# Attention's value product moved behind the next branch's scores, in one step of a woven TensorE queue

## The chip, the cores and the metric

The kernel runs on one core of a Trainium2 chip. The metric is the device time of one execution in microseconds (us), the median of several runs. One more execution was taken by the hardware profiler; its rows are quoted below. TensorE (PE in the rows), VectorE (DVE), ScalarE (ACT) and SyncE (SP) each work through a queue of their own in order, and wait for each other by semaphores.

## What is computed

The model is one hybrid layer (gated delta rule for four heads, sparse attention for four heads, a feed-forward block) and a second one (gated linear attention, a state space part, product-key experts), over 512 positions of width 1024. The change touches only the first layer's sparse attention. Per block of 128 queries and per head it has three branches, each a masked softmax, weighted by a gate, times values:

```python
s_c = jnp.einsum('bqhd,bkd->bqhk', qb, k_cmp) * scale        # 31 compressed keys
p_c = masked_softmax(s_c, mask_c[None, :, None, :])
o_c = jnp.einsum('bqhk,bkd->bqhd', p_c, v_cmp)
...                                                          # o_s: selected blocks, o_w: window
return gb[..., 0:1] * o_c + gb[..., 1:2] * o_s + gb[..., 2:3] * o_w
```

With 512 positions all eight selectable blocks are chosen and the window covers everything before a query, so both larger branches run over all keys up to the query's block. Beside it runs the gated delta rule in chunks, whose triangular system is inverted by repeated small products, and the modulation `mod = silu(c) @ ada_w + ada_b`.

## The kernel before

The mixer stage lies at 290 to 552 us of the profiled span. Three generators per engine write it down: the delta rule (`gdn_*`), attention (`attn_*`), and, inside attention's steps, the modulation (`ada_*`). `weave` draws one step of the delta rule and 0.42 steps of attention in turn (`RATES`), alike on TensorE, VectorE and ScalarE, so each engine's queue is one fixed mixture.

The delta rule has four lanes (one per chunk of 128 positions). Each lane is a chain in which TensorE makes four 128x128 products into the lane's PSUM bank (line 1102) and VectorE combines the bank with what is in SBUF (lines 1208, 1210, 1212, the matrices Y, XT and X, called `qkv` in the rows). Lanes are visited in turn, so TensorE can be three or four products ahead of VectorE. Behind the lanes follows a serial chain (`CHAIN`) over the chunks.

Attention has 48 branches: 4 query blocks `mt`, 4 heads, 3 branches `br`. At step n

- TensorE makes the scores of branch n (lines 1349 and 1352 or 1355, `bank4` or `bank5` in turn) and transposes the probabilities of branch n-2 into `bank6` (line 566);
- VectorE takes the maximum of branch n's scores (line 1415), then normalizes branch n-1 (the last of it on line 146 or 151), and does three, three or two products of a modulation tile (lines 146 and 151, `mod_acc`, in `ada_ve`);
- ScalarE takes the exponential of branch n (line 1381), then copies the transposed branch n-2 into `PC` or `PT` (lines 1390, 1392).

Every third step (n = 5, 8, ... 50) also closes a group g = (n-5)/3, which is one head of one query block. TensorE then waits for the copy of the group's last branch (`at_pt` at 3g+3), multiplies the three probability tiles with the values into a part of `bank7` (line 554 from line 1343; 1 + 2(mt+1) products), and for g > 0 ahead of it makes the modulation's two 128x1 products (`ada_pe`). ScalarE copies the result (line 1398) behind its exponential and its copy of branch n-2; that copy of branch n-2 waits for the product too, since it overwrites `PC`. VectorE subtracts what the copy lost (line 1406, `lower`), and TensorE waits for that of the group before.

A 32-bit product runs as two passes, so a product of the program is two rows' worth of the trace's counts. The stage ends when all engines have arrived (`arrive(..., 3)`), and the next one starts from there.

Of the kernel before, what the change touches and what calls it, by code (L numbers as in the profile page):

```python
# [268 lines left out]
def _build(nc, D, ctx):  # L269
    s = Sems(nc, ctx)  # L270
# [3 lines left out]
    def sb(name, shape, dt=F32, c=ctx):  # L274
        return c.enter_context(nc.sbuf_tensor(name, shape, dt))
# [24 lines left out]
    pm = bank[7]  # L300
# [21 lines left out]
    with ExitStack() as ar:  # L322
# [3 lines left out]
        tm = sb("tm", [128, 4, 276], F32, ar)  # L326
        kcmp = sb("kcmp", [128, 32], F32, ar)
        vcmp = sb("vcmp", [32, 128], F32, ar)
# [11 lines left out]
        with ExitStack() as a2:  # L340
# [4 lines left out]
            PC = sb("PC", [32, 128], F32, a2)  # L345
            PT = [sb(f"PT{j}", [128, 512], F32, a2) for j in range(2)]
# [49 lines left out]
    with ExitStack() as ar:  # L396
# [36 lines left out]
        mt = [sb(f"mt{j}", [128, 512], F32, ar) for j in range(3)]  # L433
# [118 lines left out]
    def mm(p, out, pairs, start=True, stop=True, check=True):  # L552
        for i, (l, r) in enumerate(pairs):
            ins = p.e.matmul(out, l, r, start=start and i == 0, stop=stop and i == len(pairs) - 1,  # L554
                             skip_group_check=not check)
        return ins
# [7 lines left out]
    def tr(p, out, in_):  # L564
        k = in_.shape[0]
        return p.e.transpose(out, in_, ident[0:k, 0:k])  # L566
# [152 lines left out]
    def ada_pe(p, i):  # L719
        p.wait_ge(s("ada_sum"), i + 1)  # L720
        for j in range(2):
            c = 2 * i + j
            ins = mm(p, pm[:, c:c + 1], [(mod_acc(i)[:, 128 * j:128 * j + 128], C["ones"][:, 0:1])], check=False)
        p.then_inc(ins, s("ada"))
# [600 lines left out]
    def span_of(n):  # L1325
        return 31 if branches[n][2] == 0 else 128 * (branches[n][0] + 1)

    def attn_pe(p):
        for n in range(51):
            if n >= 5 and n % 3 == 2:  # L1330
                g = (n - 5) // 3
                mt = g // 4
                if g:
                    p.wait_ge(s("at_lo"), g)
                else:
                    p.wait_ge(s("me_h"), 1)
                if g:
                    ada_pe(p, 7 + g)
                p.wait_ge(s("at_pt"), 3 * g + 3)
                pairs = [(vcmp[0:31, :], PC[0:31, 0:128])]  # L1340
                pairs += [(tm[:, j, 128 * b:128 * b + 128], PT[b][:, 128 * j:128 * j + 128])
                          for b in range(2) for j in range(mt + 1)]
                p.then_inc(mm(p, pm[:, 128:256], pairs, check=False), s("at_pv"))
            if n < 48:
                mt, h, br = branches[n]
                qT, ps, L = nsq[:, h, 128 * mt:128 * mt + 128], bank[4 + n % 2], span_of(n)
                if n >= 2:
                    p.wait_ge(s("at_ex"), n - 1)
                p.e.matmul(ps[:, 0:L], qT, kcmp[:, 0:31] if br == 0 else kk2[:, br - 1, 0:L], start=True, stop=False,
                           skip_group_check=True)  # L1350
                if br == 0:
                    ins = p.e.matmul(ps[:, 0:31], ident, C["cmpadd"][:, 31 * mt:31 * mt + 31], start=False, stop=True,
                                     skip_group_check=True)
                else:
                    ins = p.e.matmul(ps[:, L - 128:L], ident, C["causal"], start=False, stop=True, skip_group_check=True)
                p.then_inc(ins, s("at_s"))
            if 2 <= n < 50:
                m = n - 2
                P = Pb[m % 3]
                p.wait_ge(s("at_p"), m + 1)  # L1360
                if m:
                    p.wait_ge(s("at_pt"), m)
                if branches[m][2] == 0:
                    ins = tr(p, bank[6][0:31, 0:128], P[:, 0:31])
                else:
                    for j in range(branches[m][0] + 1):
                        ins = tr(p, bank[6][:, 128 * j:128 * j + 128], P[:, 128 * j:128 * j + 128])
                p.then_inc(ins, s("at_t"))
            yield
        p.wait_ge(s("at_lo"), 16)  # L1370
        ada_pe(p, 23)
# [103 lines left out]
    def mixer_pe(p):  # L1475
        arrive(p, 2)
        run(meta_pe(p))
        together((gdn_pe(p), RATES[0]), (attn_pe(p), RATES[1]))
# [1807 lines left out]
```

## Time and profile before

| | us |
|---|---|
| median of 3 runs | 3661.42 |
| lowest, highest | 3661.38, 3662.98 |
| the profiled execution's own time | 3658.62 |
| its span | 3656.7 |
| the mixer stage in it, 290.0 to 551.9 | 261.9 |

The profiled execution took 3658.62 us, of which 3656.7 are the span from the first instruction to the last and 1.9 lie around it. It is 2.8 us under the median. Over the whole span TensorE is busy for 95%, VectorE for 55% and ScalarE for 33%; these are means over stages with different limits, and the mixer stage is read by itself. A row of the timeline gives the start, the duration, the engine, the line, the operation and its tiles, and in brackets how long the engine had been idle before it and what ended that.

### The profile page before, as it was taken

What the parts mean: (1) busy time and instruction counts of PE and PEld (TensorE: products, weight loads), DVE (VectorE), ACT (ScalarE), POOL (GpSimd) and SP (SyncE); (2) the same over time, 40 slices, a digit from 0 to 9 for tenths busy, and PEclk for the clock granted to TensorE, in tenths of its full rate; (3) what the DMA queues carried; (4) which work ended last, traced back from release to release, by engine and by line L of the source; (5) the groups of instructions that cost most, each with busy time, mean ns of one, the idle gap of its engine ahead of it and who ended that gap; (6) DMA issues with size and microseconds to landing.
All of it is one profiled execution on the core that took longest, in us unless ns stands there. A gap on an engine that the chain in (4) does not pass through costs nothing.

```text
span 3656.7 us, 43203 instructions
## 1 busy us (share of the span) xinstructions
PE 3478.0 (95%) x18062; PEld 2951.6 (81%) x18062; DVE 1998.5 (55%) x3622; ACT 1217.0 (33%) x1598; POOL 0.2 (0%) x4
## 2 busy tenths in 40 slices
PE   6997879999998999999899989999999999999998
PEld 5886877878788789888787878888888888888887
DVE  6427853747434435667533288687785444444443
ACT  2234132222233324555422224444444322222222
POOL 0000000000000000000000000000000000000000
PEclk9888988999999989999998999999999999999998
DMA  5222212232321241122143333544545665555551
GB/s 222 76 88 74 81 47 92 82 109 82 119 82 54 67 158 70 58 81 92 65 176 117 147 132 125 185 157 160 186 164 179 222 233 184 196 196 184 194 196 59
DMA packets 211314, 474.64 MB, mean 130 GB/s; under 512 B 10272, under 2 KB 141856, under 8 KB 175024
## 3 DMA queue, kind: packets, MB, share of 16 engines
q1 hardware_dynamic: 208960, 463.89, 36.7%
q10 hardware_dynamic: 2160, 7.99, 0.6%
q8 instruction: 143, 2.34, 0.3%
q14 instruction: 51, 0.42, 0.0%
HBM read 380.61 MB, written 91.23 MB: 129 GB/s over the span
## 4 chain that ended last, share of the span: by engine, by line
PE 83%; DVE 9%; ACT 4%; DMA 1%; issue 1%; SPq 0%; ACTq 0%; DVEq 0%
PE bank L554 78%; PE bank L617 2%; DVE mod_acc L151 1%; DVE wl L509 1%; PE bank L2346 1%; ACT wh L502 1%; PE bank L624 1%; ACT sgm L2414 1%; DMA x<-in_xT 1%; PE bank L566 0%; DVE st L1415 0%; PE bank L1102 0%; PE bank L2355 0%; ACT P L1381 0%; ACT sgm L2418 0%
## 5 line engine op out<-in xcount | busy, mean ns | idle before, releaser
L554 PE MATMUL bank<-hh,wh 128*128 128x512 f32 (+1 forms) x2512 | 982.5, 391 | 37.1 <-DVE wl L509 13.3
L509 DVE TENSOR_TENSOR wl<-ring,wh 128x2048 fp32r<-128x2048 f32 (+2 forms) x250 | 557.1, 2229 | 817.2 <-ACT wh L502 817.1
L554 PE MATMUL bank<-hl,wh 128*128 128x512 f32 (+1 forms) x2512 | 954.8, 380 | 0.0
L554 PE MATMUL bank<-hh,wl 128*128 128x512 f32 (+1 forms) x2512 | 952.6, 379 | 0.0
L502 ACT ACTIVATE wh<-ring 128x2048 fp32r<-128x2048 f32 (+2 forms) x250 | 465.4, 1862 | 1077.9 <-PE bank L554 1070.8
L554 PEld LDWEIGHTS bank<-hh,wh 128*128 128x128 f32 x2512 | 483.8, 193 | 134.3 <-issue 32.4
L554 PEld LDWEIGHTS bank<-hl,wh 128*128 128x128 f32 x2512 | 483.1, 192 | 91.6 <-issue 6.3
L554 PEld LDWEIGHTS bank<-hh,wl 128*128 128x128 f32 x2512 | 482.0, 192 | 92.3
L554 PE MATMUL bank<-pl,wh 128*128 128x512 f32 x1024 | 403.5, 394 | 0.0
L554 PE MATMUL bank<-ph,wh 128*128 128x512 f32 x1024 | 401.4, 392 | 0.0
L554 PE MATMUL bank<-ph,wl 128*128 128x512 f32 x1024 | 397.3, 388 | 0.0
L554 PEld LDWEIGHTS bank<-ph,wh 128*128 128x128 f32 x1024 | 192.2, 188 | 45.0
L554 PEld LDWEIGHTS bank<-ph,wl 128*128 128x128 f32 x1024 | 192.2, 188 | 43.0
L554 PEld LDWEIGHTS bank<-pl,wh 128*128 128x128 f32 x1024 | 192.5, 188 | 38.2
L2803 ACT ACTIVATE stage<-bank 128x512 f32<-128x512 f32 x128 | 140.5, 1106 | 102.6 <-PE bank L554 102.6
L554 PE MATMUL bank<-wh,hh 128*128 128x256 f32 (+2 forms) x520 | 155.4, 299 | 0.0
L554 PE MATMUL bank<-wh,hl 128*128 128x256 f32 (+2 forms) x520 | 150.9, 290 | 0.0
L554 PE MATMUL bank<-wl,hh 128*128 128x256 f32 (+2 forms) x520 | 150.9, 290 | 0.0
L2884 ACT ACTIVATE gst<-bank 128x512 f32<-128x512 f32 x128 | 75.3, 590 | 204.3 <-PE bank L554 148.2
L2823 DVE TENSOR_SCALAR Ah<-cst,ijw 128x128 f32<-128x128 f32 x512 | 142.4, 342 | 0.0
L554 PEld LDWEIGHTS bank<-Bh,Ah 128*128 128x128 f32 x1024 | 133.1, 191 | 10.6
L554 PE MATMUL bank<-Bh,Ah 128*128 128x128 f32 x1024 | 133.8, 274 | 0.0
(466 smaller groups left out, 4096.2 us busy)
## 6 DMA issues: line engine op xcount, KB each, us to landing
ring<-in_v SPq DMA_DIRECT2D x68, 1024.0 KB, 4.9
ring<-in_u SPq DMA_DIRECT2D x64, 1024.0 KB, 5.5
gelu_spill<-gst SPq DMA_DIRECT2D x128, 256.0 KB, 2.4
weight_spill<-stage SPq DMA_DIRECT2D x32, 1024.0 KB, 9.0
gv<-gelu_spill SPq DMA_DIRECT2D x64, 512.0 KB, 4.4
wv<-weight_spill SPq DMA_DIRECT2D x64, 512.0 KB, 5.7
ring<-in_ada SPq DMA_DIRECT2D x24, 1024.0 KB, 5.0
ring<-in_wup SPq DMA_DIRECT2D x22, 1024.0 KB, 4.8
```

The lines of the kernel that those rows point to most:

```text
L151: return e.scalar_tensor_tensor(out=out, in0=a, scalar=x, in1=b, op0=op0, op1=op1)
L502: a.then_inc(a.e.activation(wh[q % 2][:, 0:n], ring[k % 4][:, 0:n], ACT.Copy), s("whi"))
L509: v.then_inc(v.e.tensor_tensor(wl[q % 2][:, 0:n], ring[k % 4][:, 0:n], wh[q % 2][:, 0:n].bitcast(F32), S_), s("parts"))
L554: ins = p.e.matmul(out, l, r, start=start and i == 0, stop=stop and i == len(pairs) - 1, skip_group_check=not check)
L617: ins = p.e.matmul(out[:, j:j + 1], sq[:, 128 * j:128 * j + 128], C["ones"][:, 0:1], start=start and j == 0, stop=stop, skip_group_check=True)
L624: ins = p.e.matmul(out[:, 128 * j:128 * j + 128], r[:, j:j + 1].to_broadcast([128, 128]), ident, start=j == 0, stop=True, skip_group_check ...
L2346: p.then_inc(p.e.matmul(bank[7][:, :], l, r, start=True, stop=True), s("ss_mm"))
L2414: ins = a.e.activation(sg[:, h, :], bank[3 + h // 4][:, 128 * (h % 4):128 * (h % 4) + 128], ACT.Abs, bias=nac[:, j, 8 * g + h:8 * g + h + 1])
L2803: a.then_inc(a.e.activation(stage[half][:, :, 4 * (q % 16):4 * (q % 16) + 4].rearrange("p j t -> p t j"), quad(bank[5 + t % 3][:, :]), ACT ...
L2823: ins = v.e.tensor_scalar(Ah[t % 3][:, z, :], C["iota"], ijw[:, 0, k:k + 1], ijw[:, 2, k:k + 1], ALU.is_equal, M)
L2884: a.then_inc(a.e.activation(gst[t % 2][:, :], bank[t % 4][:, :], ACT.Gelu_apprx_tanh), s("ge_u"))
```

## The change

In `attn_pe` the part that closes a group stands behind the step's scores and transposes instead of ahead of them. Nothing else is edited: the products, the tiles, the semaphores and what is waited for are the same, and so are the queues of VectorE, ScalarE and SyncE, row for row. Up to step 47 the closing part comes behind branch n's scores and branch n-2's transpose; at step 50 there are neither scores nor a transpose, and the order is as it was.

```diff
     def attn_pe(p):
         for n in range(51):
-            if n >= 5 and n % 3 == 2:
-                g = (n - 5) // 3
-                mt = g // 4
-                if g:
-                    p.wait_ge(s("at_lo"), g)
-                else:
-                    p.wait_ge(s("me_h"), 1)
-                if g:
-                    ada_pe(p, 7 + g)
-                p.wait_ge(s("at_pt"), 3 * g + 3)
-                pairs = [(vcmp[0:31, :], PC[0:31, 0:128])]
-                pairs += [(tm[:, j, 128 * b:128 * b + 128], PT[b][:, 128 * j:128 * j + 128])
-                          for b in range(2) for j in range(mt + 1)]
-                p.then_inc(mm(p, pm[:, 128:256], pairs, check=False), s("at_pv"))
             if n < 48:
...
                 p.then_inc(ins, s("at_t"))
+            if n >= 5 and n % 3 == 2:
+                g = (n - 5) // 3
+                mt = g // 4
...
+                p.then_inc(mm(p, pm[:, 128:256], pairs, check=False), s("at_pv"))
             yield
```

In the rows below `kk,nsq` are scores, `cst` with them the mask that is added, `cst,P` the transpose, `mod_acc` the modulation, `PC,vcmp` and `PT,tm` the value product. On TensorE, at step 32 (group 9, the third query block), there stood before, from the lane product ahead of the step to the one behind it:

```order
L1102 MATMUL bank<-qkv,AT 128x128 x4
L554 MATMUL bank<-cst,mod_acc_1 128x1 x2
L554 MATMUL bank<-PC,vcmp 128x128
L554 MATMUL bank<-PT,tm 128x128 x6
L1349 MATMUL bank<-kk,nsq 128x384
L1355 MATMUL bank<-cst 128x128
L566 MATMUL bank<-cst,P 31x128
L1102 MATMUL bank<-XT,Y 128x128 x4
```

and there stands now:

```order
L1102 MATMUL bank<-qkv,AT 128x128 x4
L1335 MATMUL bank<-kk,nsq 128x384
L1341 MATMUL bank<-cst 128x128
L566 MATMUL bank<-cst,P 31x128
L554 MATMUL bank<-cst,mod_acc_1 128x1 x2
L554 MATMUL bank<-PC,vcmp 128x128
L554 MATMUL bank<-PT,tm 128x128 x6
L1102 MATMUL bank<-XT,Y 128x128 x4
```

The scores and the transpose have changed places with the modulation's products and the value product; the lane products around them stay.

On TensorE at step 47 (group 14), behind the last products of the lanes (`XT,kbe` and `qkv,XT`) and ahead of the serial chain's first ones (`AT,kd` and `mix,AT`), there stood before:

```order
L1102 MATMUL bank<-qkv,XT 128x128 x4
L554 MATMUL bank<-cst,mod_acc_0 128x1 x2
L554 MATMUL bank<-PC,vcmp 128x128
L554 MATMUL bank<-PT,tm 128x128 x8
L1349 MATMUL bank<-kk,nsq 128x512
L1355 MATMUL bank<-cst 128x128
L566 MATMUL bank<-cst,P 31x128
L1102 MATMUL bank<-AT,kd 128x128 x4
```

and there stands now:

```order
L1102 MATMUL bank<-qkv,XT 128x128 x4
L1335 MATMUL bank<-kk,nsq 128x512
L1341 MATMUL bank<-cst 128x128
L566 MATMUL bank<-cst,P 31x128
L554 MATMUL bank<-cst,mod_acc_0 128x1 x2
L554 MATMUL bank<-PC,vcmp 128x128
L554 MATMUL bank<-PT,tm 128x128 x8
L1102 MATMUL bank<-AT,kd 128x128 x4
```

Here too the same pieces have changed places, and the chain's products stay behind both.

## Rows read from the trace of the kernel before

**Rows 1.** Windows of the stage: busy time per engine, granted clock, DMA share.

```profile
core 0: us, PE busy (x) PEld busy (x) DVE busy (x) ACT busy (x) POOL busy (x), PEclk, DMA share, GB/s
360.15:409.41 49.26, 44.30 (x354) 41.50 (x355) 45.62 (x125) 10.46 (x41) 0.00 (x0) 1.00 0.24 86
409.41:452.39 42.98, 37.13 (x280) 33.79 (x280) 35.21 (x94) 8.48 (x30) 0.00 (x0) 0.96 0.22 74
452.39:496.10 43.71, 37.99 (x289) 33.68 (x290) 33.02 (x88) 13.65 (x38) 0.00 (x0) 1.00 0.24 79
496.10:523.30 27.20, 23.56 (x113) 21.64 (x114) 9.00 (x25) 6.01 (x12) 0.00 (x0) 0.63 0.20 69
```

**Rows 2.** Waits of VectorE, 290 to 530 us: total, times, longest.

```profile
DVE st L1415 <- PE bank L1355: 26.3, 12, 9.5
```

**Rows 3.** Waits of TensorE, 409 to 505 us: total, times, longest.

```profile
PE bank L554 <- ACT PT L1392: 7.8, 6, 2.0
```

**Rows 4.** Timeline around the close of group 9, TensorE, VectorE and ScalarE.

```profile
422.77 0.50 PE L554 MATMUL bank<-cst,mod_acc 128*128 128x1 f32 x4
...
424.18 0.48 ACT L1392 ACTIVATE PT<-bank 128x384 f32<-128x384 f32 x1
...
424.71 0.48 PE L554 MATMUL bank<-PC,vcmp 31*128 31x128 f32 x2 [1.44 <-ACT PT L1392]
...
426.57 0.81 PE L1349 MATMUL bank<-kk,nsq 128*128 128x384 f32 x2
...
427.54 1.06 PE L1102 MATMUL bank<-XT,Y 128*128 128x128 f32 x8
...
427.63 0.56 DVE L1415 TENSOR_REDUCE st<-bank 128x1 f32<-128x384 f32 x1 [1.22 <-PE bank L1355]
...
428.42 0.58 ACT L1381 ACTIVATE P<-bank,st 128x384 f32<-128x384 f32 x1 [3.76 <-DVE st L147]
...
429.43 0.29 DVE L1406 TENSOR_TENSOR hl<-bank,hh 128x128 fp32r<-128x128 f32 x1 [0.27 <-ACT hh L1398]
```

**Rows 5.** Timeline, VectorE's maximum at the close of groups 1, 4, 8, 11 and 12.

```profile
318.76 0.29 DVE L1415 TENSOR_REDUCE st<-bank 128x1 f32<-128x128 f32 x1 [3.03 <-PE bank L1355]
...
362.42 0.42 DVE L1415 TENSOR_REDUCE st<-bank 128x1 f32<-128x256 f32 x1 [0.34 <-PE bank L1355]
...
413.92 0.56 DVE L1415 TENSOR_REDUCE st<-bank 128x1 f32<-128x384 f32 x1 [2.81 <-PE bank L1355]
...
455.53 0.69 DVE L1415 TENSOR_REDUCE st<-bank 128x1 f32<-128x512 f32 x1 [1.54 <-PE bank L1355]
...
470.56 0.69 DVE L1415 TENSOR_REDUCE st<-bank 128x1 f32<-128x512 f32 x1 [2.09 <-PE bank L1355]
```

**Rows 6.** Timeline around the close of group 13.

```profile
480.18 0.59 ACT L1392 ACTIVATE PT<-bank 128x512 f32<-128x512 f32 x1
...
480.82 0.48 PE L554 MATMUL bank<-PC,vcmp 31*128 31x128 f32 x2 [0.46 <-ACT PT L1392]
...
483.12 1.02 PE L1349 MATMUL bank<-kk,nsq 128*128 128x512 f32 x2
...
484.31 1.06 PE L1102 MATMUL bank<-qkv,XT 128*128 128x128 f32 x8
...
484.40 0.69 DVE L1415 TENSOR_REDUCE st<-bank 128x1 f32<-128x512 f32 x1 [2.09 <-PE bank L1355]
```

**Rows 7.** Timeline from the end of the lanes into the serial chain.

```profile
496.10 0.98 PE L554 MATMUL bank<-cst,mod_acc 128*128 128x1 f32 x4 [0.99 <-ACT AT L1178]
...
503.17 1.06 PE L1102 MATMUL bank<-AT,kd 128*128 128x128 f32 x8
503.26 0.69 DVE L1415 TENSOR_REDUCE st<-bank 128x1 f32<-128x512 f32 x1 [9.50 <-PE bank L1355]
...
506.80 0.68 DVE L1283 COPY St<-bank 128x512 f32<-128x512 f32 x1
...
507.54 1.16 PE L1102 MATMUL bank<-St,Y 128*128 128x128 f32 x8 [1.67 <-DVE St L1283]
```

More of the change, by code:

```diff
@@ L1368, in attn_pe @@
                 p.then_inc(ins, s("at_t"))
+            if n >= 5 and n % 3 == 2:
+                g = (n - 5) // 3
+                mt = g // 4
+                if g:
+                    p.wait_ge(s("at_lo"), g)
+                else:
+                    p.wait_ge(s("me_h"), 1)
+                if g:
+                    ada_pe(p, 7 + g)
+                p.wait_ge(s("at_pt"), 3 * g + 3)
+                pairs = [(vcmp[0:31, :], PC[0:31, 0:128])]
+                pairs += [(tm[:, j, 128 * b:128 * b + 128], PT[b][:, 128 * j:128 * j + 128])
+                          for b in range(2) for j in range(mt + 1)]
+                p.then_inc(mm(p, pm[:, 128:256], pairs, check=False), s("at_pv"))
             yield
```

## The prediction

> **What bounds the kernel now.** The change is confined to the mixer stage, so I read that stage alone, first its windows, then the waits, then the timeline around the close of a group.
>
> In the windows [rows 1] no engine has the stage to itself. From 360.15 to 409.41, VectorE is busy 45.6 of 49.3 us (93%) and TensorE 44.3. From 409.41 to 452.39 VectorE falls to 35.2 of 43.0 (82%), from 452.39 to 496.10 to 33.0 of 43.7 (76%), while TensorE is busy 37.1 and 38.0. So the second and third window each hold 8 to 11 us in which VectorE stands still, and there is no other engine that is full. That is the sign of two engines that wait for each other.
>
> The waits name the place. VectorE stands 26.3 us in 12 pieces ahead of line 1415, the maximum over a branch's scores, until TensorE's mask product of line 1355 [rows 2]. In the other direction TensorE stands 7.8 us in 6 pieces ahead of line 554 until ScalarE's copy into `PT` [rows 3]. The two belong together, as the close of group 9 shows [rows 4]: TensorE has ended the modulation's two products at 423.2 and then stands 1.44 us until the copy that began at 424.18. The value product holds it from 424.71 to 426.5, and only then come the scores, which took nothing from that copy and could have been made in the gap. VectorE, out of other work, stands 1.22 us until they are there, at 427.63.
>
> **The change part by part.** No instruction is added or removed, and only TensorE's queue is reordered. What counts is what each engine then waits for. I first follow group 9.
>
> *Scores.* They need an exponential two branches back, long done. They start where the modulation's products started, 422.8, and take 1.0 us (426.57 to 427.54, with the mask and the transpose that follow) [rows 4]. They are ready by 423.8, so VectorE's 1.22 us are gone whole. What is late next on VectorE is line 1406, which waits for ScalarE's copy of the value product.
>
> *Transpose.* It takes about 0.1 us of the queue and waits for `bank6`, that is for the same `PT` copy as the value product. It costs the value product 0.1 us.
>
> *Modulation.* Its two products, 0.5 us long and about 0.4 us of the queue [rows 4], come behind that wait now, where before they filled time ahead of it. That is the price of the change: the value product starts 0.5 to 0.6 us later against the copy than before. It ends at 427.0 to 427.1 instead of 426.5. The lane product behind it starts at about 427.1 where it was 427.54, a gain of 0.4 to 0.5 us, because the score block has left this side of the wait.
>
> *ScalarE and line 1406.* ScalarE's exponential began at 428.42 and now begins 1.22 us earlier, at 427.2; its copy of branch n-2 and the copy of the product follow from 427.8. The product is there at 427.1. So the later value product is hidden by the maximum and the exponential, by 0.7 us; if that cover were gone, every us would be one of VectorE's. Line 1406 comes 1.22 us earlier and still waits 0.27.
>
> *Who is late next.* VectorE gains 1.2 us per such group and TensorE's own order only 0.4 to 0.5, but TensorE had 1.44 us of gap in it, which it now fills with the scores and gives up. In the second window TensorE is busy 37.1 of 43.0 us [rows 1], so 5.9 us can be given up before it is the bound.
>
> The other groups, by VectorE's wait [rows 4 to 6]:
>
> - Groups 5, 6, 7 and 3 have no wait ahead of the maximum; VectorE is 93% busy there, in the first window of [rows 1]. Nothing to gain, 0. Line 1406 doesn't get later either, since the product has over 1.5 us until ScalarE comes to it.
> - Group 4: 0.34, taken as 0.3.
> - Groups 0, 1 and 2: waits of 1.2, 3.0 and 0.7 us, of which the middle one stands in [rows 5]. Here ScalarE carries the delta rule's scalings and TensorE runs at half clock around 316 to 319. The exponential is queued behind ScalarE's other work (groups 0 and 2), or TensorE is full for the next 10 us (group 1). Bounds 0 and 4.9; I take 0, since the next wait stands right behind.
> - Group 8: 2.81 [rows 5], because the product ran at half clock; the product now ends about 412.5 and delays line 1406 by some 0.15. I take 2.65.
> - Groups 9 and 10: 1.2 each.
> - Group 11: 1.54, all of it, since the gap ahead of its product was 2.0.
> - Groups 12 and 13: 2.09 each [rows 5, 6] as upper bound, 4.2. Here TensorE becomes the bound. At group 13 the gap was only 0.46 [rows 6], less than the 1.2 us of a score block with its transpose (483.12 to 484.31). From 452.4 to 491.4 TensorE's gaps come to 3.3 us (five, of which the one of 0.46 is a row), and the order itself gives it 0.6 at group 11. Following both queues on to the last lane product I get a shift of 4.3 us for groups 11 to 13, so 2.8 for groups 12 and 13. Lower bound 1.0, the two orders' own 0.5.
> - Group 14 [rows 7]: VectorE's 9.50 us of wait look like the largest prize and are not. TensorE can't start before ScalarE's last lane copy, at 496.10, and the chain's first product stands behind scores and value product in either order, at 503.17. What moves is VectorE's side: its `St` copy at 506.80 was queued behind the maximum (503.26), line 1406 and two modulation products. The maximum now comes at 498, and line 1406 waits for the value product, which ends at 503.2, so it runs at 503.8 instead of 505.3. `St` follows at 505.3, 1.5 us earlier, and TensorE's product of 507.54 with it. Bounds 0 and 1.6 (the wait of 1.67 us there); I take 1.5.
> - Group 15: the order is unchanged, 0.
>
> Sum: 0.3 + 2.65 + 1.2 + 1.2 + 1.5 + 2.8 + 1.5 = 11.15 us. From 507 on the chain is serial, and the next stage starts from an arrival of all engines, so I carry the sum to the end one for one. The modulation's sums come late by 0.6 us at most and are needed after the stage. SyncE's loads of modulation tiles wait for VectorE's sums, not for TensorE.
>
> The profiled execution would be 3658.62 - 11.15 = 3647.5; the median lies 2.8 us above it, so I predict 3661.42 - 11.2 = 3650.2.
>
> **A rule beside it.** The Trainium skill, "Perfetto Trace Analysis", section "Identifying the Most-Contended Engine", says to judge TensorE by the busy share of its weight loads and VectorE by its occupancy, and to work on whichever is higher. In the third window that makes TensorE the more contended (33.7 against 33.0 us), in the second VectorE (35.2 against 33.8). Read strictly, only TensorE's own savings would count in the third window, which is the first rival below.
>
> **Rivals.**
>
> *TensorE sets the pace.* Then VectorE's vanished waits come back ahead of its lane operations. Each group gives what the order gives TensorE: about 0.5 us in groups 9 to 13, 1.4 in group 8 (at half clock a score block is twice as long), 0.3 and 1.5 for groups 4 and 14. That is 5 x 0.5 + 1.4 + 1.8 = 5.7 us, 3655.7. For it: TensorE's 37.1 and 38.0 busy us. Against it: its gaps of 7.8 us ahead of line 554 alone [rows 3], and that it is some three lane products ahead of VectorE. 18%.
>
> *The clock gains too.* The tail from 496.10 to 523.30 ran at a granted clock of 0.63 [rows 1], about 20 us of it at 1.2 GHz, after gaps of 0.97, 1.42 and 0.99 us (the last in [rows 7]), and again from 510.5 to 522.4 after gaps of 1.67 and 1.84 us. The change shortens the 1.67. If the clock stayed at 2.4 GHz from there on, the 12 us of nearly unbroken products would take 6: 17 us in all, 3644. The same gap length was followed by full speed elsewhere, so this is open. 13%. By "TensorE: Matmul & The Clock Gate" in the Trainium skill, section "What's actually happening", the throttled state is the default and activity releases it, which speaks for this rival and against the slower one.
>
> *Slower, by the clock.* A fall of the clock is what made group 8 wait 2.81 us where groups 9 and 10 waited 1.22, so one costs 1.6 us. The new order has the same work on either side of a shorter gap, but the phase of all gaps moves. Slower by 7.3 us needs 18.5 us of loss: twelve such falls, or the window 452 to 496 at 1.2 GHz for some 40 us, when the closing product of the last query block (2.3 us) takes 4.6, outlasts the exponential, and holds line 1406 and all of VectorE's queue behind it. A gain of 11 with two or three falls is the likelier damage, 3653 to 3655. 5%.
>
> *The gain ends early.* The product's later start could hold ScalarE's copy at every group of blocks 3 and 4, which would keep VectorE's total wait and only move it to line 1406. The cover of 0.7 us at group 9 speaks against it, the lack of one at group 13 for it. It gives 0 to 4 us, 3659. 6%.
>
> **How the numbers follow.** My forecast (gains of 8 to 14 us, 3647 to 3653) has 58%. The range reaches over the first rival and half of the clock's gain: 3645 to 3657. A measurement here can tell about 0.2%, or 7.3 us, from no change, so that faster means under 3654.1. To it belong the forecast, the clock's gain and a small part of the first rival: 0.73. The same: most of the first rival, the early end, damage by a few falls: 0.22. Slower: 0.05.
>
> **What would show it.** In the profile after: VectorE's wait for line 1355 drops from 26.3 us to about 6, nearly all of it at group 14 (4 to 5, where it was 9.5) and in the first groups; its wait at line 1406 stays at 0.2 to 0.3 for groups 8 to 12 is near 1 at group 13 and near 4 at group 14. TensorE's gaps ahead of line 554 vanish, and part of them stands ahead of line 566. The `St` copy comes near 495.6 and the stage ends near 540.7. I am wrong if the waits vanish at line 1415 and turn up at lines 1208 to 1212 or 1406, or if the granted clock of 409 to 496 falls under 0.96.

## The result and the profile after

| | before | after |
|---|---|---|
| median, us (10 runs each) | 3659.7 | 3635.95 |
| lowest, highest | 3648.42, 3673.42 | 3626.42, 3649.05 |
| ratio, 95% interval | | 0.9941 (0.9927 to 0.9955) |
| the profiled execution, its span | 3658.62, 3656.7 | 3637.82, 3635.9 |

The ratio is that of the means (3658.3 and 3636.8), a gain of 21.6 us, with 16 to 27 as its interval; the two medians lie 23.8 apart. I had forecast 11.2, in a range of 3645 to 3657: the direction was right, the size half of what came, and the range missed it.

The same kernel spreads over 25 us from one execution to the next before, and over 23 after. A trace shows one draw of that, so below each stretch is read from several traces.

Where the 20.8 us between the two spans lie is best seen between the closes of groups, that is between starts of line 1406. The windows run from group 7's close to 13's, 14's and 15's. The columns are those of [rows 1]; first the kernel before:

```profile
400.41:486.43 86.02, 75.90 (x583) 68.77 (x582) 69.93 (x184) 19.31 (x64) 0.00 (x0) 0.98 0.23 76
486.43:505.29 18.86, 15.35 (x90) 13.02 (x90) 8.48 (x25) 5.75 (x16) 0.00 (x0) 0.82 0.17 57
505.29:523.81 18.52, 15.01 (x75) 14.34 (x76) 7.38 (x20) 5.17 (x9) 0.00 (x0) 0.63 0.19 58
```

and the changed kernel:

```profile
400.67:476.38 75.71, 72.32 (x571) 66.13 (x570) 69.37 (x184) 19.52 (x63) 0.00 (x0) 1.00 0.25 88
476.38:490.87 14.49, 12.14 (x94) 10.70 (x93) 8.62 (x25) 6.21 (x15) 0.00 (x0) 1.00 0.21 76
490.87:503.48 12.61, 10.19 (x87) 9.62 (x86) 7.30 (x21) 5.30 (x9) 0.00 (x0) 1.00 0.22 79
```

Groups 8 to 13 take 10.3 us less, where the sum had 9.35. The two windows behind them take 10.3 us less too (37.4 to 27.1), where the sum had 1.5. Their granted clock was 0.82 and 0.63 and is 1.00. Behind group 15 the two traces run alike (3132.9 and 3132.4 us to the end).

The close of group 9, the counterpart of [rows 4], in the timeline of the changed kernel:

```profile
420.43 0.81 PE L1335 MATMUL bank<-kk,nsq 128*128 128x384 f32 x2
...
421.54 0.48 ACT L1392 ACTIVATE PT<-bank 128x384 f32<-128x384 f32 x1
...
422.17 0.27 PE L566 MATMUL bank<-cst,P 128*31 128x128 f32 x1 [0.71 <-ACT PT L1392]
422.29 0.58 PE L554 MATMUL bank<-cst,mod_acc 128*128 128x1 f32 x4
...
422.80 0.48 PE L554 MATMUL bank<-PC,vcmp 31*128 31x128 f32 x2
...
423.70 0.55 DVE L1415 TENSOR_REDUCE st<-bank 128x1 f32<-128x384 f32 x1
...
424.65 1.06 PE L1102 MATMUL bank<-XT,Y 128*128 128x128 f32 x8
...
425.48 0.29 DVE L1406 TENSOR_TENSOR hl<-bank,hh 128x128 fp32r<-128x128 f32 x1 [0.27 <-ACT hh L1398]
```

The scores stand ahead of the copy and fill TensorE's gap. What is left of it (0.71) is now ahead of the transpose, line 566. The maximum of line 1415 has no wait in brackets any more, where it had 1.22, and line 1406 waits 0.27 as before.

The waits of VectorE in the changed kernel from 290 to 530 us, against [rows 2]; line 1341 is what was line 1355:

```profile
DVE hl L1406 <- ACT hh L1398: 15.3, 16, 3.7
DVE st L1415 <- PE bank L1341: 5.9, 3, 3.6
```

The wait ahead of the maximum fell from 26.3 to 5.9 us. That of line 1406 came to 15.0 us before and is 15.3: at group 15 it fell from 8.4 to 3.7, and at groups 1, 2 and 12 to 14 it rose. At groups 1 and 2 it rose from 0.19 and 0.57 to 1.55 and 1.32, so there part of the vanished wait only moved.

### The profile page after: what moved, and what is told of

It reads as the page before. It is cut to its first block, busy times and chain, and to the rows that moved or that the text cites. A ratio compares the mean times of both kernels' runs of the same rounds, so it can differ in the third digit from the quotient of the medians.

```text
span 3635.9 us, 43217 instructions
## 1 busy us (share of the span) xinstructions
PE 3469.8 (95%) x18062; PEld 2945.2 (81%) x18062; DVE 1997.8 (55%) x3622; ACT 1218.1 (34%) x1598; POOL 0.2 (0%) x4
## 4 chain that ended last, share of the span: by engine, by line
PE 84%; DVE 9%; ACT 4%; DMA 1%; issue 1%; SPq 0%; ACTq 0%; DVEq 0%
PE bank L554 78%; PE bank L617 2%; DVE mod_acc L151 1%; DVE wl L509 1%; PE bank L1102 1%; PE bank L2346 1%; ACT wh L502 1%; PE bank L624 1%; ACT sgm L2414 1%; DMA x<-in_xT 1%; PE bank L566 0%; PE bank L2355 0%; ACT sgm L2418 0%; ACT L2418 0%; DMA s_<-score_spill 0%
## 5 line engine op out<-in xcount | busy, mean ns | idle before, releaser
L554 PE MATMUL bank<-hh,wh 128*128 128x512 f32 (+1 forms) x2512 | 983.6, 392 | 37.2 <-DVE wl L509 13.5
```

## The experiments

Each kernel is compared with the kernel before on its own chip. The table gives ratios, where there is more than one execution, and from each kernel's one trace the time between closes: from group 7 to 13, and the tail from 13 to 15, whose second part, 14 to 15, is also given alone.

| kernel | ratio (95%) | 7 to 13 | 13 to 15 | 14 to 15 |
|---|---|---|---|---|
| before | | 86.0 | 37.4 | 18.5 |
| before, again | | 90.0 | 37.1 | 18.4 |
| after | 0.9941 (0.9927 to 0.9955) | 75.7 | 27.1 | 12.6 |
| after, again | 0.9954 (0.9937 to 0.9971) | 75.7 | 27.1 | 12.6 |
| step 47 alone | 0.9987 (0.9975 to 0.9999) | 86.1 | 30.5 | 12.6 |
| all but step 47 | 0.9965 (0.9953 to 0.9977) | 76.4 | 37.5 | 18.5 |
| steps 29 to 44 alone | 0.9974 (0.9965 to 0.9983) | 76.4 | 37.6 | 18.5 |
| steps 5 to 26 alone | 1.0003 (0.9990 to 1.0016) | 88.5 | 37.2 | 18.5 |
| before, five bursts | 0.9981 (0.9969 to 0.9993) | 90.0 | 28.2 | 12.6 |
| before, burst at the St gap | 0.9993 (0.9981 to 1.0004) | 90.0 | 33.2 | 17.4 |
| the same, again | one run | 86.0 | 31.5 | 12.6 |
| before, burst at the 1.84 us gap | one run | 90.0 | 28.4 | 12.6 |
| before, bursts at both | one run | 86.1 | 31.3 | 12.6 |
| before, three bursts at the lanes' end | 0.9995 (0.9985 to 1.0006) | 86.1 | 32.3 | 16.7 |
| after, five bursts | 0.9936 (0.9921 to 0.9950) | 75.7 | 27.2 | 12.6 |
| modulation early | 0.9947 (0.9933 to 0.9962) | 75.3 | 30.7 | 12.6 |
| value product ahead of the transpose | 0.9947 (0.9935 to 0.9959) | 75.0 | 33.5 | 15.9 |
| modulation early, five bursts | 0.9928 (0.9911 to 0.9945) | 75.3 | 27.2 | 12.6 |

### Which steps carry the gain

Four kernels place the closing part by a condition on n, here for step 47 alone; the block stands a second time behind the transposes under the opposite condition:

```diff
-            if n >= 5 and n % 3 == 2:
+            if n >= 5 and n % 3 == 2 and n != 47:
...
+            if n >= 5 and n % 3 == 2 and not (n != 47):
```

> The new order at step 47 alone (group 14); steps 5 to 44 as before. In the two profiled executions the groups up to 13 brought 10 to 11.6 us, as summed, and the stretch from step 47 to group 15's close 10.3 us, of which the sum has 1.5; the rest lies in the granted clock there (0.63 before, 1.00 after). Theory A (the tail's clock gain belongs to the order of step 47 itself): 8 to 11 us faster than before, ratio about 0.9974, tail at full clock. Theory B (the clock of the tail comes out differently because everything ahead of it moved, or by chance from one execution to the next): 1.5 us faster, ratio 0.9996, tail at 1.2 GHz as often as before.

> The new order at all closing steps except step 47. By the sum: groups 4 to 13 give 9.65 us, ratio 0.9974. Theory A (clock gain by step 47's order): that and no more. Theory B1 (clock gain by the groups ahead of it): 18 to 20 us, ratio 0.9948. Theory B2 (the clock varies by chance in each kernel alike): 10 us on the mean.

The windows of step 47 alone, groups 13 to 14 and 14 to 15:

```profile
483.49:501.36 17.87, 14.60 (x77) 12.22 (x77) 8.47 (x26) 5.82 (x15) 0.00 (x0) 0.76 0.17 60
501.36:513.95 12.59, 11.01 (x89) 10.68 (x88) 7.28 (x20) 5.30 (x9) 0.00 (x0) 0.94 0.23 79
```

and of all but step 47:

```profile
479.18:498.20 19.02, 16.47 (x104) 14.40 (x103) 8.61 (x25) 6.13 (x16) 0.00 (x0) 0.82 0.16 59
498.20:516.72 18.52, 15.02 (x75) 14.35 (x76) 7.38 (x21) 5.17 (x9) 0.00 (x0) 0.63 0.17 58
```

With the old order at step 47, everything ahead may have moved by 9 us and the tail still has 37.5 us and a clock of 0.63 in its second part. With the new order at step 47 alone that part takes 12.6 us. So the clock gain of the second part goes with step 47's own order (theory A), and not with what stands ahead (B1). Its size in time is 4.8 us by the ratio (0.4 to 9), at the lower edge of theory A's 8 to 11. The first part of the tail, groups 13 to 14, was slow in both traces (0.76 and 0.82), and is taken up again below. All but step 47 gives 12.8 us (8 to 17); the 9.65 of the sum lies within. The two parts add up to 17.6 us against 21.6 for the whole change, a difference that these intervals can't tell from none.

> The new order at steps 29 to 44 alone (groups 8 to 13), where VectorE's waits add up to 11.0 us in the trace of before and the sum has 9.35. Expected 9 to 10 us faster than before, ratio 0.9974, the tail's clock as in the kernel before, so that it measures like the kernel with every closing step but 47 (0.9965). If the early groups carry part of that gain it stays at 6 us or less.

> The new order at steps 5 to 26 alone (groups 0 to 7). By the sum 0.3 us, ratio 1.000; upper bound 4.9 + 0.3 us, 0.9986. VectorE's waits ahead of line 1415 of groups 1 and 2 go and come back at line 1406.

Steps 29 to 44 alone give 9.5 us (6 to 13), as expected; groups 8 to 13 take 76.4 us in the trace. Steps 5 to 26 alone can't be told from no change. In its trace group 3 closes 57.4 us after the start of the reciprocal of line 1409, against 59.7 before. VectorE's waits ahead of the maximum at groups 1 and 2 are gone and come back in part at line 1406 (1.56 and 1.36 us), as expected. But groups 8 to 13, which have the old order there, drew 88.5 us instead of 86.0.

### What the clock of the tail hangs on

Bursts of products whose results nobody uses keep TensorE at work where it would wait:

```diff
+    def filler(p, b):
+        for _ in range(4):
+            p.e.matmul(bank[b][:, 0:128], ident, ident, start=True, stop=True, skip_group_check=True)
...
+            if at in (("wS", 1), ("kV", 1)):
+                filler(p, 3)
```

The five-burst kernels have it also ahead of the fourth lane's `w` and `u` and ahead of `lanes_read`.

> The order before, and five bursts of four 128x128 products (0.9 us each at 2.4 GHz) of the identity into a bank that nobody reads, put ahead of TensorE's waits in the tail: ahead of the fourth lane's last two products, ahead of the serial chain, and ahead of its second and third product, where TensorE stood 0.97, 1.42, 0.99, 1.67 and 1.84 us. Their results are not used. If the tail's clock falls because of these gaps, the tail runs at 2.4 GHz with them and the kernel gains up to 9 us less 0.5 for what bursts overlap: ratio 0.9975 to 0.998. If the clock there doesn't hang on these gaps, it is up to 1 us slower.

```profile
487.62:503.25 15.63, 14.91 (x114) 13.16 (x114) 8.47 (x26) 5.74 (x16) 0.00 (x0) 1.00 0.20 69
503.25:515.85 12.60, 10.88 (x91) 10.36 (x92) 7.29 (x20) 5.16 (x9) 0.00 (x0) 1.00 0.22 81
```

These are its two windows of the tail. In the old order, with nothing else changed, the tail takes 28.2 us at full clock. That prices the slow clock at 37.4 - 28.2 = 9.2 us, and step 47's order by itself at 28.2 - 27.1 = 1.1 us. Both are differences of single traces. The ratio of the kernel with bursts gives 6.9 us (2.6 to 11).

> The changed kernel with the same five bursts; the difference to the kernel before with bursts is then what the order brings at like clock in the tail. If the changed kernel's tail mostly runs at 2.4 GHz by itself, it measures as the changed kernel does, ratio 0.994, or up to 1 us more. If the clock of the tail is chance in the changed kernel too, it gains some us on it, ratio 0.992.

It took 23.4 us off (18 to 29), which can't be told from the changed kernel's 21.6. In both of its own traces the changed kernel holds the clock through the tail by itself, and there the bursts had nothing to give.

> The order before, with one burst of four unused 128x128 products ahead of TensorE's wait for the chain's first state (the gap of 1.67 us ahead of the product that reads St). In the four traces with the old order at step 47 and no burst, groups 13 to 15 lie 37.1 to 37.6 us apart, with two stretches at 1.2 GHz (6.8 and 13.7 us); in the four with the new order 27.1, 30.5, 30.7 and 33.5, and the 13.7 us stretch is in none. Theory: it is this gap, which the new order shortens to 0.6, that brings the second stretch. Then the burst alone removes it and leaves the first: groups 13 to 15 about 31 us apart, though VectorE's state copy comes no earlier; 6 us off the whole. If the second stretch hangs on something else, 37 us remain.

> The order before, with three bursts ahead of the gaps of 0.97, 1.42 and 0.99 us at the end of the lanes and none in the chain. Theory (each slow stretch follows its own gaps): the first one (6.8 us) goes, which is worth 3 us, and the second (13.7 us) stays: groups 13 to 15 some 34 us apart. If the second were a consequence of the first, both go and 28 us remain, as with all five bursts (28.3).

The first didn't go as my theory said. With the burst at the St gap alone, it was the first slow stretch that was missing, and a slow one followed the gap of 1.84 us all the same. TensorE in that kernel:

```profile
505.53 1.16 PE L1102 MATMUL bank<-St,Y 128*128 128x128 f32 x8 [0.77 <-DVE St L1290]
508.53 1.16 PE L1102 MATMUL bank<-kbe,kd 128*128 128x128 f32 x8 [1.84 <-DVE kbe L1285]
...
511.49 0.78 PE L1102 MATMUL bank<-qkv,St 128*128 128x128 f32 x2
```

The last row's product takes 0.78 us where it takes 0.47 at full clock. The second went as the theory said: with the lanes' end filled the first stretch is gone and the second stayed, though shorter (16.7 us), 32.3 us in all where 34 were expected. Since one trace of each can't settle it, four more executions were profiled, one of each kernel.

> The order before, with one burst of four unused products ahead of the chain's second state update (the gap of 1.84 us), none elsewhere. If either gap of the chain is enough to bring the second stretch at 1.2 GHz, it stays, and groups 14 and 15 lie 16 to 18.5 us apart (18.5 before, 17.4 with the other gap filled). If it hangs on the 1.84 us gap alone, 12.6.

> The order before, with both gaps of the chain (1.67 and 1.84 us) filled and the lanes' end left as it was. If the two gaps together bring the second stretch, it is gone: groups 14 and 15 lie 12.6 us apart, and the first stretch stays or not by its own gaps. If all five bursts were needed, 16 to 18.5.

> The kernel before once more, for a second trace. If the second stretch belongs to the old order, groups 14 and 15 lie 18.4 to 18.6 us apart again, as in all four traces with that order and no burst. If it is chance, they may lie 12.6 apart.

> The order before with the burst ahead of the St gap alone, for a second trace. The first had groups 14 and 15 17.4 us apart. If it is at 12.6 now, one burst keeps the clock in some executions and not in others; if at 17 again, the gap of 1.84 us is enough to lose it in the old order.

The kernel before again and the St gap filled again, each from group 14's close to 15's:

```profile
507.80:526.21 18.41, 14.90 (x75) 14.24 (x76) 7.37 (x20) 5.16 (x9) 0.00 (x0) 0.63 0.16 58
```

```profile
502.41:515.01 12.60, 9.99 (x83) 9.47 (x84) 7.28 (x20) 5.17 (x9) 0.00 (x0) 1.00 0.24 79
```

The 1.84 us gap filled alone, with TensorE's two gaps:

```profile
510.36 1.16 PE L1102 MATMUL bank<-St,Y 128*128 128x128 f32 x8 [1.67 <-DVE St L1290]
...
513.35 1.16 PE L1102 MATMUL bank<-kbe,kd 128*128 128x128 f32 x8 [0.94 <-DVE kbe L1285]
...
515.60 0.47 PE L1102 MATMUL bank<-qkv,St 128*128 128x128 f32 x2
```

Counted over all traces, groups 14 and 15 lie 18.4 to 18.5 us apart in five of five with the old order at step 47 and no burst, and 16.7 with bursts only at the lanes' end. With one or both of the chain's gaps shortened by a burst they lie 12.6 apart in four of five (17.4 in the fifth). With the new order they lie 12.6 apart in six of seven, with bursts or without, and 15.9 in the seventh. So neither gap alone decides. The two together lose the clock in each of these traces, and with either one shortened it is mostly kept. Why it fell in one trace with a short St gap and in another of the same program did not was not tried further.

The first slow stretch, between the closes of groups 13 and 14, is a different matter. With the old order at step 47 and no burst at the lanes' end it came in seven of nine traces (18.6 to 19.1 us) and not in the other two (15.8 us); in these two the only bursts stand behind it in the queue, so they can't have kept it away. With the new order at step 47 and no burst it came in three of five (17.7 to 18.1 us), and both traces of the changed kernel are among the two without it (14.5 us). TensorE's waits ahead of it were alike either way. The products at the lanes' end, first in the trace of the kernel before again, where the clock fell:

```profile
496.66 1.16 PE L1102 MATMUL bank<-qkv,XT 128*128 128x128 f32 x8 [1.42 <-ACT Y L1176]
498.82 0.98 PE L554 MATMUL bank<-cst,mod_acc 128*128 128x1 f32 x4 [1.00 <-ACT AT L1178]
```

and in that with the burst at the St gap, where it did not:

```profile
495.01 1.16 PE L1102 MATMUL bank<-qkv,XT 128*128 128x128 f32 x8 [1.42 <-ACT Y L1181]
497.17 0.58 PE L554 MATMUL bank<-cst,mod_acc 128*128 128x1 f32 x4 [0.99 <-ACT AT L1183]
```

So this stretch isn't shown to hang on the order of step 47. With bursts at the lanes' end it is absent in four of four.

The kernel before with five bursts has the same two products behind gaps of 0.77 and 0.95 us, and a clock of 1.00 in the window shown above; the kernel before has 1.67 and 1.84 us ahead of them, and 0.63. By the Trainium skill, "TensorE: Matmul & The Clock Gate", section "What's actually happening", the throttled state is the default and activity releases it: in direction these traces agree. They don't give a rule for a single gap.

### Where the closing part could stand otherwise

> The changed kernel, but the modulation's two products stay ahead of the wait: scores, modulation, transpose, value product. The prediction priced their move behind the wait for the copy at 0.4 us of TensorE's queue a group. Theory: VectorE is the bound up to group 11, so nothing comes of it there; in groups 12 and 13, where TensorE was late and line 1406 waited 0.65 and 1.2 us, up to 0.4 us each; together 0.5 to 1 us under the changed kernel, which the comparison can't tell, but the waits at line 1406 of groups 12 and 13 shrink to about 0.3 and 0.8. If TensorE were the bound all along, 15 x 0.4 = 6 us less.

```profile
460.20 0.29 DVE L1406 TENSOR_TENSOR hl<-bank,hh 128x128 fp32r<-128x128 f32 x1 [0.30 <-ACT hh L1398]
...
472.71 0.29 DVE L1406 TENSOR_TENSOR hl<-bank,hh 128x128 fp32r<-128x128 f32 x1 [1.16 <-ACT hh L1398]
```

Its line 1406 waits 0.30 us at group 12, where the changed kernel has 0.65, and 1.16 at group 13, where I expected 0.8 and nothing changed. Groups 8 to 13 take 75.3 us against 75.7: groups 8 to 11 are the same to 0.01 us, and group 12 is 0.35 shorter. So up to group 11 VectorE sets the pace, and the modulation's products cost next to nothing behind the wait. TensorE is close behind: it is busy for 72.3 of the 75.7 us in the changed kernel.

> The closing part behind the step's scores but ahead of its transpose. Scores still fill the gap, so the gain by VectorE's waits is the same; the value product comes 0.1 us earlier and ScalarE's copy of branch n-2 isn't later, since it waits for the product anyway. Expected to measure like the changed kernel, ratio 0.994; if the place of the transposes mattered, it would lie between that and 1.

As expected for the ratio, and groups 8 to 13 take 75.0 us. The place of the transpose makes no difference that can be told; that of the scores carries the gain. Its tail drew 33.5 us.

> The changed kernel once more, for a second trace and a second mean: groups 8 to 13 take 75.7 us as in the first trace (86.0 before), since they run at 2.4 GHz in both; groups 13 to 15 between 27 and 34, without the stretch of 13.7 us. Ratio 0.994.

Both traces of the changed kernel give the same 75.7, 14.5 and 12.6 us. That is two draws; the two kernels just above, which differ from it little, had slow stretches in the tail.

> Scores, modulation, transpose, value product, and the five bursts in the tail: the candidate for the fastest. Each part alone measured as the changed kernel within what can be told. The bursts fix the tail at 27 us where the new order alone has 27 to 34 (mean 30.5), so 3 us on the mean, and the modulation's place 1 to 2: 3 to 5 us under the changed kernel, ratio 0.993.

It has the lowest ratio of all, 0.9928, but its interval holds the changed kernel's 0.9941 and overlaps that of its second measurement. It is well below the kernel before, and not shown to be better than the change.

## Why the prediction fell short

Averages over traces with the same order in a stretch show the parts. Up to the close of group 3, from the start of line 1409: 59.9 us in ten traces of the old order, 58.5 in five of the new. Groups 4 to 7: 50.5 and 50.3. Groups 8 to 13: 87.9 in ten and 76.0 in five. Tail, without bursts: 37.4 in five and 28.2 in three. The gains are 1.4, 0.2, 11.9 and 9.2, together 22.7 us, and 21.6 were measured. The forecast had 0, 0.3, 9.35 and 1.5. Of the some 11.5 us that it lacks against these averages, 7.7 lie in the tail and 2.5 in groups 8 to 13.

**Groups 8 to 13: the mechanism was right.** VectorE's waits ahead of the maximum vanished, one by one. From close to close, groups 8 to 13 gained 2.9, 1.3, 1.3, 1.6, 1.8 and 1.3 us in the first pair of traces; the terms were 2.65, 1.2, 1.2, 1.5 and 2.8 for the last two, which brought 3.1. The limit of TensorE showed one group earlier than it was put: line 1406 waits 0.27 to 0.31 us up to group 11, then 0.65 and 1.20, where the forecast had 0.2 to 0.3 up to group 12 and about 1 at group 13. At group 13, as forecast, TensorE had no gap left and the value product ended behind the exponential:

```profile
473.36 0.48 PE L554 MATMUL bank<-PC,vcmp 31*128 31x128 f32 x2
473.47 0.68 DVE L1415 TENSOR_REDUCE st<-bank 128x1 f32<-128x512 f32 x1
...
475.93 0.27 ACT L1390 ACTIVATE PC<-bank 31x128 f32<-31x128 f32 x1 [0.77 <-PE bank L554]
...
476.38 0.29 DVE L1406 TENSOR_TENSOR hl<-bank,hh 128x128 fp32r<-128x128 f32 x1 [1.20 <-ACT hh L1398]
```

What the sum left out are falls of the clock. In four of ten traces the old order has groups 8 to 13 at 90.0 and in one at 88.5 instead of 86.0, with a window clock of 0.92 to 0.94. None of the eight with the new order there exceeds 76.4. I had read one trace, which happened to be one of the five at 86.0, as if it were the kernel. The kernel before again, groups 8 to 13:

```profile
399.15:489.15 90.00, 80.53 (x583) 72.84 (x582) 69.93 (x184) 19.31 (x64) 0.00 (x0) 0.92 0.21 73
```

VectorE and ScalarE are busy for as long as in the first trace, to 0.01 us; TensorE's same products take 4.6 us longer.

**Groups 0 to 7.** The value 0 for groups 0 to 2 was too low: it was 1.4 on the mean, inside my bounds of 0 and 4.9, but in the trace of all but step 47 group 3 closed at 60.8 us, later than in any with the old order. In the first pair of traces group 4 gained 0.4 (0.3 in the sum) and group 5 lost 0.7, and groups 4 to 7 together brought nothing; the mean of 50.5 owes its 0.2 to one trace at 52.1.

**Group 14 and the chain: the step that failed.** VectorE's side came about as worked out: the maximum moved ahead, `St` was no longer late behind it, and this is worth the 1.1 us measured at full clock, near the 1.5. But I carried the sum from there to the end "one for one", at the clock that the trace of before had, so that the clock's share of the tail stood at nothing in the sum; it measured 8.1 us on the mean (9.2 less 1.1). After it, with the new order:

```profile
487.51 0.69 DVE L1415 TENSOR_REDUCE st<-bank 128x1 f32<-128x512 f32 x1 [3.62 <-PE bank L1341]
...
492.38 0.68 DVE L1283 COPY St<-bank 128x512 f32<-128x512 f32 x1
...
493.12 1.16 PE L1102 MATMUL bank<-St,Y 128*128 128x128 f32 x8 [0.58 <-DVE St L1283]
...
496.12 1.16 PE L1102 MATMUL bank<-kbe,kd 128*128 128x128 f32 x8 [1.84 <-DVE kbe L1278]
```

These are the changed kernel's rows against [rows 7]. The gap ahead of the product with `St` went from 1.67 to 0.58 us and the one behind it stayed at 1.84, and what follows runs at 2.4 GHz, where it ran at 1.2 GHz for 12 us. On the mean the part from group 14 to 15 takes 12.6 instead of 18.5 us, and this 5.9 is shown to go with step 47's order. The part from 13 to 14 takes 15.6 instead of 18.9; about 1 of these 3.3 us is the order's, and the rest is the first slow stretch, whose absence stays unexplained. That the forecast took the slow clock for granted shows in its signs too: line 1406 was to wait near 4 us at group 14. It waits 1.64 at full clock, and 4.1 in the traces of step 47 alone and of the modulation early, where the first stretch was slow.

I had the second stretch as the rival "the clock gains too", with its place and 17 us as its result, and gave it 13%, because gaps of like length elsewhere had been followed by full speed. The gaps in question were two in a row, 3.5 us of standing within 5 us, and I weighed each by itself. Its step from 12 us to 6 was right in size, but its 17 us in all still fell short of the 21.6, since it too left out the first stretch and the falls in groups 8 to 13. The first rival (TensorE sets the pace, 5.7 us) is excluded by groups 8 to 13; in groups 12 and 13 it allowed 1.0 us, and 3.1 came. The early end of the gain is excluded there too, since line 1406's waits stayed as they were up to group 11. The slower one did not occur: clock falls became fewer.

## What to carry to other kernels

When a part moves in a queue, ask two things of the work it now lets through: which engine's wait goes (read off the timeline, group by group, it came within 1 us here for groups 8 to 13 of the first pair of traces), and which gaps of TensorE it shortens. Where the trace shows TensorE at 1.2 GHz behind a run of gaps, and the change shortens one of them, the clock is a term of the sum and not a remote rival. Price it from a stretch of the same work at full clock: here 12.6 us, against 18.5 at the slow one.

One trace is one draw of the clock. Groups 8 to 13 came out at 86.0 us in one trace and at 90.0 in another of the same program, twice (the kernel before, and that with a burst at the St gap). So take a second trace before a stretch's clock is built into a sum.

## What the runs showed of the hardware

Work that nobody needs can pay on TensorE when it keeps the clock. With five bursts of four unused products in the gaps of the tail, the same chain took 28.2 us in its trace instead of 37.4, with 20 products more, and the program gained 6.9 us (2.6 to 11). A single burst at the St gap, or three at the lanes' end, can't be told from no change by their ratios (0.9993 and 0.9995), and in the changed kernel, whose two traces had no slow stretch in the tail, the five bursts brought nothing that can be told.

Equal waits did not bring an equal clock. Behind the same waits of 1.42 and 0.99 to 1.00 us at the lanes' end the granted clock fell in one trace and stayed in another.
